# A two-block transformer kernel: the first block cut into two token blocks between the state rows and the routing, its norms fused, its modulation chunks moved

## The reference

```
mod = (c_act @ w_mod + b_mod)                      # 6 x 1024: sh1 sc1 gt1 sh2 sc2 gt2
y = (y_diag + y_off + d_skip * xs)                 # rows of the state-space part
g = y * silu(z);  g = g * rsqrt(mean(g^2) + eps)
y_ssd = (g * ssd_norm_w) @ w_ssd_o
merged = sigmoid(g_ssd) * y_ssd + sigmoid(g_att) * y_att
x = layer_norm(alpha * x + (1 + gt1) * (merged @ w_o), ln1_g, ln1_b)
h = layer_norm(x) * (1 + sc2) + sh2
logits = h @ w_router                              # picks 2 of 16 experts for each token
out = sum over experts of gate * ((silu(h @ w_gate) * (h @ w_up)) @ w_down)
```

## Time and profile before

| | |
|---|---|
| median of 3 runs | 1845.14 us (1840.89 to 1846.67) |
| the profiled execution's own time | 1839.81 us |
| its span in the profile | 1837.8 us |
| PE busy | 1694.2 us (92%) |
| DVE busy | 920.6 us (50%) |
| ACT busy | 634.0 us (34%) |
| DMA | 333.27 MB, mean 181 GB/s |
| granted TensorE clock, mean | 0.962 |

### The profile page before, as it was taken

One profiled execution on the slowest core, in us unless ns is written; L12 is line 12 of the kernel. 1 busy time (PEld: TensorE's weight loads), 2 busy tenths in 40 slices (PEclk: granted clock), 3 DMA queues, 4 the chain that ended last, 5 costly groups with the idle time before them and its releaser, 6 DMA issues.

```text
span 1837.8 us, 22292 instructions
## 1 busy us (share of the span) xinstructions
PE 1694.2 (92%) x9383; PEld 1296.2 (71%) x9383; DVE 920.6 (50%) x1291; ACT 634.0 (34%) x919; POOL 23.0 (1%) x81
## 2 busy tenths in 40 slices
PE   4899989996999997989999989999979999989998
PEld 1897657444443435858788879987857778879996
DVE  4586234426111115536557556654536657556653
ACT  0454211000000003426564454433436564444442
POOL 1000001000000000000000000000000000000000
PEclk9799888996999998999999999999999999999999
DMA  7355331367699995441334435554441324535552
GB/s 256 139 184 184 136 117 67 110 246 285 248 411 410 410 410 182 165 137 47 138 115 165 163 96 189 190 193 153 165 167 55 138 108 145 183 103 184 184 184 92
DMA packets 165246, 333.27 MB, mean 181 GB/s; under 512 B 17571, under 2 KB 69029, under 8 KB 165157
## 3 DMA queue, kind: packets, MB, share of 16 engines
q1 hardware_dynamic: 159312, 325.89, 48.8%
q10 hardware_dynamic: 5846, 6.11, 1.0%
HBM read 330.94 MB, written 1.05 MB: 181 GB/s over the span
## 4 chain that ended last, share of the span: by engine, by line
PE 73%; DVE 11%; DMA 9%; ACT 4%; issue 2%; POOL 0%; SPq 0%; POOLq 0%; DVEq 0%; ACTq 0%
PE ps_g L680 19%; PE ps_g L661 18%; DMA arena<-in_w_up_dram 6%; PE ps_g L1084 5%; PE ps_g L967 4%; PE ps_s L1278 3%; PE ps_p L1278 3%; PE ps_o L735 3%; DVE ring_r L1896 2%; DMA ring<-in_w_mod_dram 2%; PE ps_x L634 2%; PE ps_s L706 1%; PE ps_s L661 1%; PE ps_p L661 1%; PE ps_g L767 1%
## 5 line engine op out<-in xcount | busy, mean ns | idle before, releaser
L1896 DVE TENSOR_TENSOR ring_r<-ring,late_w 128x4096 fp32r<-128x4096 f32 (+1 forms) x50 | 216.9, 4338 | 148.6 <-ACT late_w L1522 148.6
L1522 ACT ACTIVATE late_w<-ring 128x4096 fp32r<-128x4096 f32 (+1 forms) x50 | 178.0, 3560 | 126.7 <-PE ps_p L1278 42.9
L680 PE MATMUL ps_g<-h_t_r,late_w 128*128 128x256 f32 x640 | 180.0, 281 | 0.0
L680 PE MATMUL ps_g<-hf_high,ring_r 128*128 128x256 f32 x640 | 179.0, 280 | 0.0
L680 PE MATMUL ps_g<-hf_high,late_w 128*128 128x256 f32 x576 | 161.7, 281 | 0.0
L967 PE MATMUL ps_g<-ring,arena 128*64 128x512 f32 x384 | 112.2, 592 | 10.4 <-DMA arena<-in_w_up_dram 8.9
L680 PEld LDWEIGHTS ps_g<-hf_high,ring_r 128*128 128x128 f32 x640 | 121.0, 189 | 0.0
L680 PEld LDWEIGHTS ps_g<-h_t_r,late_w 128*128 128x128 f32 x640 | 120.6, 188 | 0.0
L680 PEld LDWEIGHTS ps_g<-hf_high,late_w 128*128 128x128 f32 x576 | 108.4, 188 | 0.0
L967 PEld LDWEIGHTS ps_g<-ring,arena 128*64 128x64 f32 x384 | 35.8, 137 | 81.7 <-issue 81.7
L1546 ACT ACTIVATE arena<-arena,neg_max 128x256 f32<-128x256 f32 (+1 forms) x160 | 71.5, 449 | 61.5 <-DVE neg_max L1948 61.5
(11 more groups left out here) (616 smaller groups left out, 3739.5 us busy)
## 6 DMA issues: line engine op xcount, KB each, us to landing
ring<-in_w_in_dram SPq DMA_DIRECT2D x31, 2048.0 KB, 7.6
ring<-in_w_gate_up_dram SPq DMA_DIRECT2D x44, 1024.0 KB, 7.1
ring<-in_w_gate_dram SPq DMA_DIRECT2D x16, 2048.0 KB, 16.8
arena<-in_w_down_dram SPq DMA_DIRECT2D x16, 2048.0 KB, 14.7
ring<-in_w_mod_dram SPq DMA_DIRECT2D x12, 2048.0 KB, 9.9
ring<-in_w_down_dram SPq DMA_DIRECT2D x10, 2048.0 KB, 7.7
ring<-in_w_up_dram SPq DMA_DIRECT2D x8, 2048.0 KB, 18.1
arena<-in_w_up_dram SPq DMA_DIRECT2D x8, 2048.0 KB, 22.8
```

What stands on the lines that cost most here:

```text
L680: ins = pe.matmul(b.ap[:, (f % 2) * SEQ:(f % 2 + 1) * SEQ], a[:, k, f * P:(f + 1) * P], x[:, k, :], start=k == 0 and i == 0, stop=k == nk ...
L1522: act.activation(high_of(name, rnd)[:, 0:n], ring[:, slot, 0:n], ACT.Copy).then_inc(high_ready.sem, 1)
L1896: dve.tensor_tensor(ring_r[:, slot, 0:n], ring[:, slot, 0:n], high_of(name, rnd)[:, 0:n].bitcast(F32), ALU.subtract).then_inc(low_ready.se ...
```

## The change

Six edits are made together.

1. Token blocks. The gated norm, both transposes, the products with so and o, the merge, the residual, both layer norms and the transposes of h are done for token block 0 and then for block 1, with the work of one block beside that of the other. A bank of PSUM now belongs to a half of the columns instead of a token block. `turn_block` and `copy_block` turn one block in two banks of four pieces. `y_turned` is now `h_t`, and the merged rows are turned into a new view, `mg_turned`. POOL's roots are taken for each block.
2. Norms. (x - mean) * rstd, then * gain, then + shift (three operations) become (x - mean) * gain, and then * rstd + shift (two).
3. h in two operations. The same for the scale and shift of h; the columns of the modulation are stored in the order that the strided h needs (`by_pair`), so the strided read is only of x.
4. mod4 is made by DVE (`add_modulation(4)`, before the state rows) instead of PE.
5. mod5, mod6, mod7 in groups of 32 lanes: each of the eight products has 32 broadcast columns instead of 128, and piece k goes to lanes 32 * (k mod 4); ACT copies the four strips, and one product with a column that has ones in lanes 0, 32, 64, 96 sums them.
6. mod10 and mod11 come forward. Their DVE sums stand in and behind the attention, their chunks ahead of `att` and `gs1`, and PE's part stands ahead of h's transposes and behind the router's product.

```diff
-MOD_SUMMED = [0, 2, 8, 9, 10, 11]
-FIRST_CHUNKS = (... "ga1", "mod8", "gs0", "mod9", "att", "gs1",
-                "mod4", "so0", "so1", "mod10", "mod5", "o0", "o1", "mod11", "mod6", "mod7"])
+MOD_SUMMED = [0, 2, 8, 9, 10, 11, 4]
+FIRST_CHUNKS = (... "ga1", "mod8", "gs0", "mod9", "mod10", "att",
+                "mod11", "gs1", "mod4", "mod5", "so0", "so1", "o0", "o1", "mod6", "mod7"])
...
+            def mod_strips(i):
+                name, b = MOD_CHUNKS[i], mod_bank(i)
+                w = keys(chunk(pe, "first", name), KD, HALF)
+                claim(b, f"{name}s")
+                for k in range(KD):
+                    lanes = slice(32 * (k % 4), 32 * (k % 4) + 32)
+                    ins = pe.matmul(b.ap[lanes, :], c_act[:, k:k + 1].broadcast_to([P, 32]), w[:, k, :], start=k < 4, stop=k >= 4)
+                ins.then_inc(b.full, 1)
+                used["first", name] = (b, f"{name}s")
+
+            def strips_sum(i):
+                b = mod_bank(i)
+                claim(b, MOD_CHUNKS[i])
+                pe.wait_ge(consts, 2)
+                pe.matmul(b.ap[:, 0:HALF], strip_head[:, 0:1].broadcast_to([P, P]), mod_cols(i), start=True, stop=False)
+                modulation_end(i)
...
+            mod_strips(5)
+            inside(0)
+            strips_sum(5)
+            modulation(4)
             ...
+            inside(1)
+            gy_block(0)
+            block_turned("gy", 0)
+            product_block("so0", 0, y_turned)
+            gy_block(1)
+            product_block("so1", 0, y_turned)
+            block_turned("gy", 1)
+            product_block("so0", 1, y_turned)
+            mg_block(0)
+            product_block("so1", 1, y_turned)
+            block_turned("mg", 0)
+            product_block("o0", 0, mg_turned)
+            mg_block(1)
+            product_block("o1", 0, mg_turned)
+            block_turned("mg", 1)
+            product_block("o0", 1, mg_turned)
+            product_block("o1", 1, mg_turned)
+            mod_strips(6)
+            mod_strips(7)
+            strips_sum(6)
+            strips_sum(7)
             modulation(10)
+            for tb in range(TB):
+                pe.wait_ge(rows.sem, rows.at("first", f"h2_{tb}"))
+                turn_block("h2", tb, lambda k: h_rows[:, tb, k * P:(k + 1) * P])
...
             product_rows("first", "route", "route", h_t, route_w, KD, 0, N_GROUPS + N_EXPERTS)
+            modulation(11)
...
+            def normed(tb):
+                moments(tb, f"ln1_{tb}")
+                st.done(dve.scalar_tensor_tensor(x_rows[:, tb, :], resid[:, tb, :], mean_var[:, tb, 0:1], ln_rows[:, 0, :], ALU.subtract, ALU.mult))
+                ...
+                st.done(dve.scalar_tensor_tensor(x_rows[:, tb, :], x_rows[:, tb, :], rstd[:, tb:tb + 1], ln_rows[:, 1, :], ALU.mult, ALU.add))
+                ...
+                moments(tb, f"h2_{tb}")
+                for s in range(2):
+                    st.done(dve.scalar_tensor_tensor(paired(h_rows[:, tb, :], s), x_rows[:, tb, :]..., mean_var[:, tb, 0:1], paired(mod[:, 4, :], s), ALU.subtract, ALU.mult))
```

## The result

The changed kernel takes 1799.22 us (median of 4 runs, 1798.13 to 1800.25), the kernel before beside it 1843.58 (median of 4, 1840.89 to 1846.67): a ratio of 0.9771, with a 95% interval of 0.9745 to 0.9797. It is 44 us faster. The prediction had 1815 and a range down to 1804, so the gain is larger than the range allowed. The profiled execution took 1800.25 us, with a span of 1798.3 and a mean granted clock of 0.967, against 1839.8, 1837.8 and 0.962.

The account below looks back on a forecast made before the run. PE, or what PE waits for, was taken as the bound between 302 and 467 us; -1.5 - 10.0 - 15.7 - 3.4 + 0.7 = -29.9 gave 1809.9 profiled, 1815 with 5.3 added for the median; range 1804 to 1831.

Parts of the forecast that it names:

- stage 1: State rows, mod4 and gated norm until the first product with so0: 33.4 us before, gain 1.5 forecast, mostly half clock.
- Strips: Eight 32-column matmuls each for mod5, mod6 and mod7 on PE: 2.0 us forecast, against 7.0 with no overlap.
- Stage 2: Eight products with so and o, with their transposes: 71.5 us before, 61.5 forecast, including 2.2 for a half-clock start.
- Stage 3: DVE alone, from the last residual product to turned rows: 27.7 us before, 12.0 forecast, level with the copy of mod7.
- Stage 4: Transposes, copies and the router's product: 11.5 us before, gain 3.4 forecast, with 5.5 for the router's product.
- Stage 5: Picking and gathering until the first expert product: 20.4 us before, loss of 0.7 forecast for mod11's copy on DVE.
- The hole for mod11's chunk: PE's wait of 2.5 us among the products with so and o, forecast to go.
- Strips without overlap: Rival: 32-column matmuls do not overlap, so mod5, mod6 and mod7 cost 14 us more: 1829; chance 0.11.
- Clock low in stages 1 and 2: Rival: PE's clock stays low behind waits, needing two products each time, with slow `yd1`: 1827; chance 0.11.
- Half clock throughout the products: Rival: all eight products with so and o at half clock, net 23 us slower: 1868; chance 0.04.
- Given back in the loop: Rival: the expert loop waits for its first pair's weights and loses the whole gain: 1845; chance 0.03.

Follow-up runs that it names:

- p1_chunks: Kernel before with only the new chunk order, mod4 on DVE, and the DVE sums of mod10 and mod11 moved ahead; 1838.07 us, ratio 0.9967.
- p3_norms: Kernel before with only the two norms of the stretch made in two operations per block, gain and shift inside; 1837.67 us, ratio 0.9974.
- c1: Changed kernel with the strips of mod5 moved behind `yd0`, so that `yd0` waits for its bank again; 1803.18 us.
- f1: Changed kernel with strips of mod5 and sum of mod4 behind gy's block 0, sum of mod5 behind the products with so; 1796.87 us, ratio 0.9774.
- b1: Kernel before with mod4 moved ahead of `yd0` on PE, into the wait of 0.86 us; 1851.20 us, ratio 1.0041.
- d1: Changed kernel with the strips of mod5 behind `yd0` and two useless 128x512 matmuls in the wait ahead of it; 1802.17 us.
- g1: Changed kernel with mod4's sum behind gy's block 0, mod5's behind mg's block 0, and DVE turning block 0 before taking `yd1`; 1789.15 us, ratio 0.9703.
- a1_wide: Changed kernel with mod5, mod6 and mod7 as full 128-lane products instead of strips; 1811.11 us, ratio 0.9839.

## Why the prediction was too high

**The step that failed is stage 1's clock term.** It put `yd0` at 6.3, the sums at 3.7 each, `yo` at 3.6 and `yd1` at 5.2, all of them mostly or wholly at half clock. They took 3.6, 2.1 and 2.1, 1.8 and 3.5, by the starts of the rows: 9.3 us less. Before, the clock fell in `yd0`, behind a wait of 0.86. The prediction wrote in the same line that the strips fill this wait, and kept the low clock all the same, as if the thin products alone brought it down. All profiles speak against that: the fifteen `yd` groups with no wait ahead took 3.7 to 3.8 us, and the nine behind a wait of 0.8 to 1.3 us took 5.5 to 7.1. Of these nine, six are falls of the clock (`yd0` of the kernel before, p1_chunks, p3_norms, c1 and f1, and b1's `yd1`); the other three, `yd1` in the first three of these, only found it still at 0.50. c1 and d1, alike but for two useless products in the wait, show that filling the wait keeps the clock, and g1, whose three thin groups follow each other without a wait, that no wide product is needed between them.

**Its bound failed too.** The prediction gave a gain of 6 for stage 1 at full clock throughout. Its own terms at full speed are 2.0 + 3.5 + 2.0 + 2.0 + 1.9 + 3.5 = 14.9 against the 24.5 it used, a gain of 1.5 + 9.6 = 11.1, and 11.0 was measured. With this bound, and the prediction's other terms, the low end would have been 1799, level with the measured time.

**The two ends of the sum.** The median missed by some 16 us: 9.6 in the profiled execution and 6.3 beside it. 5.3 us were added because the median shown stood that much above the profiled execution. That was scatter: the kernel before had medians of 1839.7 to 1844.4 here, and the changed kernel's own profiled run, 1800.25, lies 1.0 above its median, which makes up the 6.3. Against 1809.9 for the profiled execution the error is 9.6: stage 1 gave 9.5, stages 2 and 4 0.9 and 1.0, the front 1.5; the rest gave back 3.3, which is within its scatter of 7 us.

**Point by point.** Strips: 1.92 for eight 32-lane matmuls by the row, 2.0 forecast; a full-width chunk takes 7.13 in a1_wide, so all four groups overlap (7.13 / 1.92 = 3.7). That is near the "up to 4×" that the Trainium skill, TensorEngine Tiling (Array Packing), section Theoretical Speedup, gives, and the drain that its section Key Properties names costs nothing that the rows show: `yd0` starts 1.86 us after the strips, with no wait. Stage 2: 60.6 against 61.5, although the half clock of the first product cost 3.07 instead of 2.2. Stage 3: 12.0, and DVE did not wait for ACT; that the two were level was right, since ACT's copy of mod7 ended at 393.34 and DVE's operation that needs it began at 393.47, and since a1_wide waited 7.87 for it. Stage 4: 7.1, since the router's product took 4.79 and not 5.5; that is luck, as it took 3.72 to 6.04 in the seven profiles of the changed kernel and its variants with blocks. Stage 5: right. The hole for mod11's chunk: gone, 2.5, shown by p1_chunks. mod4 on DVE: the 6 us are worth nothing by themselves (p1_chunks); that they pay with the token blocks, which take DVE's work off the end of stage 1, is argued and no run shows it.

**The rivals.** Strips without overlap: refuted. Clock low in stages 1 and 2: the opposite happened in stage 1; in stage 2 one product was slow, not two. Half clock throughout the products: refuted, 0.95 over stage 2. Given back in the loop: no. The loop began 42.8 us earlier and the span ended 39.5 earlier; the 3.3 between are within the 7 us over which the rest scatters.

**What the parts are worth**, by the stretch: chunks alone 0 (164.5 to 164.6); norms alone 6.4, of which 5.8 lie in stage 3 and the rest is what the clock gave and took elsewhere (the router's product 4.09 instead of 6.99, the products with so 29.35 instead of 27.70); chunks, norms and strips together 14.4; token blocks on top 26.9. The parts move the wait to another engine: the chunks alone left PE waiting for DVE, the norms alone left DVE waiting for PE. The strips were only taken out of the whole (a1_wide, 13.4), not put in alone.

## What to carry to other kernels

When work is put into a wait, ask what clock the products behind the wait had, and price them at the speed that they will have without it: here waits of 0.86 and 1.31 us had some 8 us of half clock behind them (5.47, 7.09, 3.73 and 7.87 where full speed gives 3.7, 3.6, 1.9 and 7.1), and even useless products in such a wait paid, with 2.7 us inside stage 1, though the time of the program could not show it. Work a bound out from the same terms as the sum, at their extreme values, and not by feel. And judge an edit to one stretch of a long kernel by that stretch in the trace, which came out within 0.7 us in the one repeat, when the whole program scatters by more; and look into the stretch for pieces that changed though the edit did not touch them, as the router's product did in f1_fill.

## What the runs showed of the hardware

Waits of 0.78 to 1.32 us with 128x64 matmuls behind them took the granted clock from 1.00 to 0.50 in all six cases in which it had been at 1.00: within 1.1 to 1.8 us of the start of `yd0` in five, and at the end of the wait itself in b1_mod4_ahead. A wait of 0.98 us ahead of a 128x512 product (f1_fill) did not, and neither did one of 2.54 us in the kernel before; one of 3.36 us in b1_mod4_ahead did. PE, before and then in b1_mod4_ahead:

```profile
393.28 13.97 PE L661 MATMUL ps_g<-ring,h_t 128*128 128x512 f32 x32 [2.54 <-DVE arena L2275]
...
395.32 16.75 PE L661 MATMUL ps_g<-ring,h_t 128*128 128x512 f32 x32 [3.36 <-DVE arena L2275]
```

Behind the wait of 4.27 us the first product took 8.80 to 9.99 us instead of 7.1 in five profiles. The router's product, 128x20 and behind a wait of 1.04 us, shows the thin case again: in the changed kernel the clock was at 1.00 when it began and at 0.50 from 400.8 to 417.8.

The Trainium skill, TensorE: Matmul & The Clock Gate, section HAM oscillation, explains such falls by idle gaps of TensorE between groups of matmuls; the wait of 4.27 agrees with it, but by idle time alone the waits of 0.98 and 1.13 us in f1_fill should do the same as each other, and they did not. What it is about the thin products that adds to the wait was not tried by itself.
